# Negated scores, one joined map, and sliced head norms between attention rounds

## The reference, cut to what matters

```
logits = einsum('bqhmd,bkhmd->bhmqk', q_blk, k) + bias      # m = 0, 1: two maps a head
p = softmax(logits)
attn = p[:, :, 0] - lam * p[:, :, 1]
o = einsum('bhqk,bkhd->bqhd', attn, v)                      # 128 columns a head
o = o * rsqrt(mean(o * o, axis=-1) + 1e-5) * subln_g * (1 - lam_init)
```

```
score = where(admissible, einsum(w, relu(q_idx @ k_idx)), -inf);  sel = top_k(score, 128)
p = softmax(q . k[sel] / 8);           y_a = p @ v[sel]
qb, kb = rms_norm(qb, qn_b), rms_norm(kb, kn_b)            # per head of 64 columns
p = softmax(qb . kb / 8 + bias);       y_b = p @ vb
```

## Time and profile before

| | us |
|---|---|
| median of three runs | 4347.05 |
| span of the profiled execution | 4333.6 |
| PE busy in it | 3912.4 (90%) |
| DVE busy | 1669.4 (39%) |
| ACT busy | 1415.7 (33%) |
| POOL busy | 1391.7 (32%) |

### The profile page before, as it was taken

One profiled execution on the slowest core, in us unless ns is written; L12 is line 12 of the kernel. 1 busy time (PEld: TensorE's weight loads), 2 busy tenths in 40 slices (PEclk: granted clock), 3 DMA queues, 4 the chain that ended last, 5 costly groups with the idle time before them and its releaser, 6 DMA issues.

```text
span 4333.6 us, 66123 instructions
## 1 busy us (share of the span) xinstructions
PE 3912.4 (90%) x28400; PEld 3137.0 (72%) x28400; DVE 1669.4 (39%) x2914; ACT 1415.7 (33%) x2424; POOL 1391.7 (32%) x583
## 2 busy tenths in 40 slices
PE   7898789989989897989999979889899898898999
PEld 5687568878766786668777867668688676676887
DVE  4443340367133443241465147633211357322112
ACT  3344152222223343252222223442322224533222
POOL 4000324434333001314444434214344344033443
PEclk9899799999999998999999989989999999899999
DMA  3000212247321001212265222012222221121222
GB/s 131 2 3 5 80 43 99 96 166 255 110 78 39 3 3 41 76 49 97 78 244 197 93 78 78 30 49 98 92 91 85 97 78 39 40 92 67 95 97 97
DMA packets 37147, 356.59 MB, mean 82 GB/s; under 512 B 4224, under 2 KB 4352, under 8 KB 17920
## 3 DMA queue, kind: packets, MB, share of 16 engines
q1 hardware_dynamic: 19584, 278.93, 17.3%
q10 hardware_dynamic: 17280, 73.48, 4.8%
HBM read 350.29 MB, written 2.10 MB: 81 GB/s over the span
## 4 chain that ended last, share of the span: by engine, by line
PE 80%; DVE 11%; ACT 4%; issue 2%; POOL 1%; DMA 1%; POOLq 0%; DVEq 0%; PEldq 0%; ACTq 0%; SPq 0%; PEld 0%
PE bank L683 21%; PE bank L684 21%; PE bank L685 21%; PE bank L1013 12%; PE bank L1989 3%; ACT arena L2139 2%; ACT arena L1343 1%; DVE arena L1788 1%; DVE arena L1691 1%; DVE arena L2454 1%; DVE arena L2453 1%; DVE x L1851 1%; DMA ring<-stream 1%; POOL small L2299 1%; ACT hi_ring L762 1%
## 5 line engine op out<-in xcount | busy, mean ns | idle before, releaser
L771 POOL TENSOR_TENSOR ring_r<-ring,hi_ring 128x1024 fp32r<-128x1024 f32 (+1 forms) x522 | 1278.1, 2453 | 2556.1 <-ACT hi_ring L762 2556.1
L683 PE MATMUL bank<-xT_r,ring_r 128*128 128x512 f32 x2288 | 924.1, 404 | 24.0 <-DVE x_lo_r L2525 17.7
L684 PE MATMUL bank<-x_lo_r,hi_ring 128*128 128x512 f32 x2288 | 911.2, 398 | 0.0
L685 PE MATMUL bank<-xT_r,hi_ring 128*128 128x512 f32 x2288 | 906.7, 396 | 0.0
L762 ACT ACTIVATE hi_ring<-ring 128x1024 fp32r<-128x1024 f32 (+1 forms) x522 | 543.8, 1046 | 797.1 <-PE bank L685 356.1
L683 PEld LDWEIGHTS bank<-xT_r,ring_r 128*128 128x128 f32 x2288 | 440.0, 192 | 132.7 <-issue 31.3
L685 PEld LDWEIGHTS bank<-xT_r,hi_ring 128*128 128x128 f32 x2288 | 437.2, 191 | 102.7
L684 PEld LDWEIGHTS bank<-x_lo_r,hi_ring 128*128 128x128 f32 x2288 | 439.4, 192 | 95.5 <-issue 1.8
L1013 PE MATMUL bank<-arena 64*64 64x64 f32 (+4 forms) x7456 | 397.2, 250 | 77.6 <-DVE arena L1691 29.6
L1343 ACT ACTIVATE arena<-bank 128x512 f32<-128x512 f32 (+1 forms) x422 | 230.6, 548 | 568.7 <-PE bank L685 360.8
L1013 PEld LDWEIGHTS bank<-arena 64*64 64x64 f32 (+2 forms) x7456 | 307.4, 140 | 134.4 <-issue 91.6
(11 more groups left out here) (250 smaller groups left out, 5038.5 us busy)
## 6 DMA issues: line engine op xcount, KB each, us to landing
ring<-stream SPq DMA_DIRECT2D x132, 2048.0 KB, 7.8
arena<-ada ACTq DMA_DIRECT2D x96, 512.0 KB, 4.4
arena<-ln_rows ACTq DMA_DIRECT2D x5, 1024.0 KB, 7.6
arena<-edge ACTq DMA_DIRECT2D x4, 1024.0 KB, 5.0
arena<-edge ACTq DMA_DIRECT2D x2, 1792.0 KB, 7.6
arena<-pack ACTq DMA_DIRECT2D x2, 1485.0 KB, 6.1
arena<-pack ACTq DMA_DIRECT2D x2, 1200.5 KB, 12.6
x<-x_in SPq DMA_DIRECT2D x4, 512.0 KB, 7.4
```

Of the source, the lines that this page charges most:

```text
L683: first = nc.tensor.matmul(out_, left[1], right[0], start=start, stop=False)
L684: low = nc.tensor.matmul(out_, left[0], right[1], start=False, stop=False)
L685: return first, low, nc.tensor.matmul(out_, left[0], right[0], start=False, stop=stop)
L771: nc.gpsimd.tensor_tensor(feed.raw(n, ring_r), feed.raw(n), feed.hi(n).bitcast(F32), ALU.subtract).then_inc(split_lo, 1)
```

## The change

In block 1 and block 2, DVE's reduction now writes the negated sum of score and bias and keeps its minimum, which is the negated maximum; the separate negation goes, and ACT's exponential takes a scale of -1 and waits for the bank to be drained. In block 1 map 0 is no longer scaled: map 1 is scaled by -lambda times the ratio of the two row sums and added, and the missing factor is applied when ACT copies the output out of PSUM. ACT's Square of each output with its row sum goes; in its place `att_norm` begins with one Square of all 2048 columns on ACT and one reduction on DVE. In block 2 only 4 of the 18 steps of the last search stand ahead of the attentions, and the others follow one a round in rounds 0 to 13. The head norm of qb goes into rounds 0 to 10; kb's squares are in rounds 5 to 8 (before 1, 3, 5, 7), its eps in 9 (before 8), its multiplications in 12 to 15 (before 10 to 13), and it has cells of its own for the sums.

```diff
...
@@ -73,6 +73,7 @@
 FT2 = 22
 TOPK = 128
 TOP_STEPS = TOPK // 8 + 2
+TOP_EARLY = 4
 HQ = 8
 NEG = -1.0e30
 TAKEN = -3.0e38
@@ -445,10 +446,6 @@
             add("rows_T", name, c, banks=(banks[c % len(banks)],))
     rest = [(name, i, tt) for name in ("qb", "kb", "vb") for i in range(4) for tt in range(TT)]
 
-    def head_late(what, proj, n):
-        for tt in range(n):
-            add("head_" + what, proj, tt)
-
     def more(n):
 
         for name, i, tt in rest[:n]:
@@ -483,29 +480,27 @@
             add("idx", qt, h, banks=(h % 2,))
             if h in (3, 5):
                 more(1)
-        for i in range(TOP_STEPS if qt < TT - 1 else TOP_STEPS // 2):
+        for i in range(TOP_STEPS if qt < TT - 1 else TOP_EARLY):
             add("top", qt, i)
         more((10, 18, len(rest))[qt - 1])
-    head_late("sq", "qb", TT)
-    add("head_eps", "qb", banks=("power",))
-    head_late("mul", "qb", TT)
 
     def attend(a):
         for n in range(2):
             add("s_qk", a, n, banks=(2 + n,))
-        top, part = TOP_STEPS // 2, 16 * a
+        top, part = TOP_EARLY, 16 * a
         for n in range(TT * HQ + 3):
             if n < TT * HQ:
                 add("s_soft", a, n)
-            while a == 0 and top < min(TOP_STEPS, TOP_STEPS // 2 + TOP_STEPS * (n + 1) // 28):
+            while a == 0 and top < min(TOP_STEPS, TOP_EARLY + n + 1):
                 add("top", TT - 1, top)
                 top += 1
-            if a == 0 and n in (1, 3, 5, 7):
-                add("head_sq", "kb", n // 2)
-            if a == 0 and n == 8:
-                add("head_eps", "kb", banks=("power",))
-            if a == 0 and n in (10, 11, 12, 13):
-                add("head_mul", "kb", n - 10)
+            for proj, at_ in (("qb", 0), ("kb", 5)) if a == 0 else ():
+                if at_ <= n < at_ + TT:
+                    add("head_sq", proj, n - at_)
+                if n == at_ + TT:
+                    add("head_eps", proj, banks=("power",))
+                if at_ + 7 <= n < at_ + 7 + TT:
+                    add("head_mul", proj, n - at_ - 7)
             if 2 <= n < TT * HQ + 2:
                 add("s_tr", a, n - 2, banks=((4, 0)[n % 2],))
             if part < (16, 24)[a]:
@@ -938,6 +933,7 @@
     o_tok = region(20388, TT)
     prob = [region(a_, 2) for a_ in (22436, 23460, 8548, 9572)]
     probT = region(24484, 2)
+    o_squares = region(24484, TT)
     pool_tmp = region(25508, 2, S + 2 * PAD)
     merged = region(10664, DT)
     gates = region(14760, DT)
@@ -961,7 +957,8 @@
     subln_s = tiny(1)
     neg_lam = tiny(4)
     row_sum = tiny(2 * 16)
-    row_max = tiny(2 * 16)
+    minus_max = tiny(2 * 16)
+    power_kb = tiny(32)
     row_w = tiny(2 * 16)
     sq_sum = tiny(32)
     power = tiny(32)
...
@@ -1459,10 +1456,10 @@
                 f(v[:, i, :], bank[b][:, :], ACT.Copy).then_inc(bank_free[b], 1)
             elif name == "att_soft":
                 i = args[0]
-                act.wait_ge(scores_ready, i + 1)
                 for m in range(2):
                     k = 2 * i + m
-                    ins = f(prob[i % 4][:, m, :], prob[i % 4][:, m, :], ACT.Exp, bias=row_max[:, k:k + 1],
+                    drained(act, uses, "att_qk", i, only=m)
+                    ins = f(prob[i % 4][:, m, :], prob[i % 4][:, m, :], ACT.Exp, bias=minus_max[:, k:k + 1], scale=-1.0,
                             accum_out=row_sum[:, k:k + 1])
                 ins.then_inc(exp_done, 1)
             elif name == "att_tr":
@@ -1473,8 +1470,11 @@
                 i = args[0]
                 h, qt = i // TT, i % TT
                 filled(b, n)
-                f(pool_tmp[:, i % 2, 0:P], bank[b][:, 0:P], ACT.Square, accum_out=sq_sum[:, i:i + 1])
-                f(o_tok[:, qt, h * P:(h + 1) * P], bank[b][:, 0:P], ACT.Copy).then_inc(bank_free[b], 1)
+                f(o_tok[:, qt, h * P:(h + 1) * P], bank[b][:, 0:P], ACT.Copy, scale=row_w[:, 2 * i:2 * i + 1]).then_inc(bank_free[b], 1)
+            elif name == "att_norm":
+                for i in (DH * TT - 2, DH * TT - 1):
+                    drained(act, uses, "att_pv", i)
+                f(o_squares.rearrange("p t c -> p (t c)"), o_tok.rearrange("p t c -> p (t c)"), ACT.Square).then_inc(o_squared, 1)
             elif name == "att_out":
                 h = args[0]
                 filled(b, n)
@@ -1786,28 +1786,26 @@
                     filled(banks[m], use[m])
                     at_ = (TT - 1 - qt) * P
                     V.tensor_tensor_reduce(out=prob[i % 4][:, m, :], in0=bank[banks[m]][:, :], in1=rel[:, h, at_:at_ + S],
-                                           scale=1.0, scalar=-3.0e38, op0=ALU.add, op1=ALU.max,
-                                           accum_out=row_max[:, k:k + 1]).then_inc(bank_free[banks[m]], 1)
-                again(banks[1], use[1])
-                V.tensor_scalar(row_max[:, 2 * i:2 * i + 2], row_max[:, 2 * i:2 * i + 2], -1.0, None, ALU.mult)\
-                    .then_inc(scores_ready, 1)
+                                           scale=-1.0, scalar=3.0e38, op0=ALU.add, op1=ALU.min,
+                                           accum_out=minus_max[:, k:k + 1]).then_inc(bank_free[banks[m]], 1)
             elif name == "att_tr":
                 i = args[0]
                 dve.wait_ge(exp_done, i + 1)
                 w = row_w[:, 2 * i:2 * i + 2]
                 link(V.reciprocal(w, row_sum[:, 2 * i:2 * i + 2]))
-                link(V.tensor_tensor(w[:, 1:2], w[:, 1:2], neg_lam[:, 0:1], ALU.mult))
+                link(V.scalar_tensor_tensor(out=w[:, 1:2], in0=w[:, 1:2], scalar=neg_lam[:, 0:1], in1=row_sum[:, 2 * i:2 * i + 1],
+                                            op0=ALU.mult, op1=ALU.mult))
                 p0, p1 = prob[i % 4][:, 0, :], prob[i % 4][:, 1, :]
-                link(V.tensor_scalar(p0, p0, w[:, 0:1], None, ALU.mult))
                 V.scalar_tensor_tensor(out=p0, in0=p1, scalar=w[:, 1:2], in1=p0, op0=ALU.mult, op1=ALU.add)\
                     .then_inc(prob_ready, 1)
             elif name == "att_norm":
-                for i in (DH * TT - 2, DH * TT - 1):
-                    drained(dve, uses, "att_pv", i)
-                V.tensor_scalar(power[:, 0:16], sq_sum[:, 0:16], 1.0 / P, 1e-5, ALU.mult, ALU.add).then_inc(stats_ready, 1)
+                dve.wait_ge(o_squared, 1)
+                link(V.tensor_reduce(power[:, 0:16].rearrange("p (t h) -> p t h", t=TT),
+                                     o_squares.rearrange("p t (h c) -> p t h c", h=DH), AX.X, ALU.add))
+                V.tensor_scalar(power[:, 0:16], power[:, 0:16], 1.0 / P, 1e-5, ALU.mult, ALU.add).then_inc(stats_ready, 1)
                 dve.wait_ge(power_ready, n + 1)
                 V.tensor_tensor(o_tok.rearrange("p t (h c) -> p t h c", h=DH), o_tok.rearrange("p t (h c) -> p t h c", h=DH),
-                                power[:, 0:16].rearrange("p (h t) -> p t h", h=DH).unsqueeze(3).to_broadcast([P, TT, DH, P]),
+                                power[:, 0:16].rearrange("p (t h) -> p t h", t=TT).unsqueeze(3).to_broadcast([P, TT, DH, P]),
                                 ALU.mult).then_inc(o_scaled, 1)
             elif name == "branch":
                 k, dt = args
...
@@ -2226,8 +2223,8 @@
                 a, i = args
                 qt, h = i // HQ, i % HQ
                 w = (qt + 1) * P
-                act.wait_ge(score2_ready, a * TT * HQ + i + 1)
-                f(prob2[a][:, i % 4, 0:w], prob2[a][:, i % 4, 0:w], ACT.Exp, bias=row_max[:, i:i + 1],
+                drained(act, uses, "s_qk", a, i)
+                f(prob2[a][:, i % 4, 0:w], prob2[a][:, i % 4, 0:w], ACT.Exp, bias=minus_max[:, i:i + 1], scale=-1.0,
                   accum_out=sum2[:, i:i + 1]).then_inc(exp2_done, 1)
             elif name == "s_tr":
                 a, i = args
@@ -2294,7 +2291,7 @@
             if "power" not in banks:
                 return
             n = use[banks.index("power")]
-            cell = power[:, args[1]:args[1] + 1] if name == "rms" else power[:, 0:width[args[0]]]
+            cell = power[:, args[1]:args[1] + 1] if name == "rms" else (power_kb if args[0] == "kb" else power)[:, 0:width[args[0]]]
             pool.wait_ge(stats_ready, n + 1)
             nc.gpsimd.tensor_tensor(cell, cell, half_minus.to_broadcast([P, cell.shape[1]]), ALU.pow).then_inc(power_ready, 1)
         return step
...
@@ -2382,16 +2383,17 @@
             elif name == "head_sq":
                 proj, tt = args
                 dve.wait_ge(sums_sq, 2 + TT * HEADS_LATE.index(proj) + tt)
-                link(V.tensor_reduce(power[:, tt * HQ:(tt + 1) * HQ], stage_sq[proj][:, tt, :].rearrange("p (h c) -> p h c", h=HQ),
+                link(V.tensor_reduce(power_of(proj)[:, tt * HQ:(tt + 1) * HQ], stage_sq[proj][:, tt, :].rearrange("p (h c) -> p h c", h=HQ),
                                      AX.X, ALU.add))
             elif name == "head_eps":
-                V.tensor_scalar(power, power, 1.0 / CH, EPS2, ALU.mult, ALU.add).then_inc(stats_ready, 1)
```

(21 more changed lines are left out.)

## The result

The changed kernel takes 4299.07 us (median of 4 executions, 4292.79 to 4306.14), the one before 4346.57 (median of 4): a ratio of 0.9894 (95% interval 0.988 to 0.9908), 47.5 us faster. A second comparison gave 4299.89 against 4343.51, 43.6 faster. The two intervals put the gain between 39 and 52 us. Forecast was 4313, 34.2 us faster, with a range down to 4302: the direction and most terms were right, the gain was larger than the range allowed.

A forecast was written before the change was run, and what follows sets the result against it. Mostly PE matmuls bound the kernel, with DVE pacing block 1's rounds; only stretches where PE waits change. Block 2's -30.0 and block 1's -4.2 make -34.2 us: 4313, with 4302 to 4331 holding about 8 in 10.

The forecast's parts named there:

- Block 2's start: Block 2's first reduction, freed of five search steps and qb's norm, starts at 2720.2 instead of 2736.61: -16.4 us.
- The first 14 rounds: Block 2's first 14 rounds take on moved search and norm work: 39.0 us, against 34.9 today.
- Block 1's rounds: Block 1's attention: the period falls from 2.99 us to PE's 2.60, bounds 2.30 and 2.75.
- Block 1's norm: Behind block 1's rounds, ACT's Square and DVE's reduction now stand bare ahead of the power: +4.1 us per layer.
- Block 1 in all: Block 1's rounds and norm together: -2.1 us per layer, -4.2 for both, bounds +3 and -13.
- A: Block 2, round 10: kb's power holds qb's multiplication 3.4 us, twice; 4320 us, chance 0.12.
- B: Block 2's first 14 rounds: DVE idles 6.3 us again; 4322, or 4325 with the negation's gain halved; chance 0.14.
- C: Block 1's rounds: scores pack tighter, period falls to DVE's 2.3; 4301 us with no idle in block 2; chance 0.10.
- D: Block 2's first 14 rounds: the loop goes in series with the moved work; slower, 4360 us, chance 0.05.
- Block 2, the later rounds: Block 2's chain from 2772 to 2896 loses the negation 15 times at 0.18: 2.7 us per layer, bounds 0 and 3.5.
- My +4.1: Growth forecast for block 2's first 14 rounds, from 34.9 us today to 39.0.
- the closing step: End of block 2's search, counted as DVE work in the first 14 rounds: 2.7 us, 2.22 and a short one.

The follow-up runs named there:

- its experiment: Block 1's part of the change alone, block 2 as before, against the kernel before: 4339.46 us, ratio 0.9992 (0.9983 to 1.0002).
- the spread search: Changed kernel with five search steps ahead of block 2's first scores, the other thirteen at three for five rounds: 4294.6 us, ratio 0.9892.

## Why the prediction missed

**Right in place and size.** *Block 2's start*: -16.4 forecast. The first reduction comes 22.1 us earlier than before, of which 5.7 were there already (the first search's first `MAX8` starts at 2644.39 instead of 2650.05), so -16.4. *The first 14 rounds*: 39.0 forecast, 38.03 measured; DVE's work 37.0 forecast, 36.71 measured. PE's busy time in them didn't shrink as the forecast said: the clock rose from 0.83 to 0.96, but 166 matmul records fall into the stretch instead of 145, and 32.35 became 34.04. *Block 1's rounds*: 2.60 forecast, 2.63 measured, set by PE as said, though PE's wait for the joining instruction isn't gone but stands in every other round. *Block 1's norm*: +4.1 forecast; PE's wait grew from 6.30 to 10.38, by 4.1. Block 1 in all -2.1 per layer forecast; from the first reduction to the output transposes it is 56.96 before and 54.86 after, -2.1, and -4.05 for both layers by its experiment's medians. Two outer bounds of the working are added up wrong (2 × 8.0 is 16, not 18, for block 2; 2 × 6.0 is 12, not 13, for block 1); neither entered the range.

**Rivals.** A, B, C and D fell. *A*: kb's power and qb's fourth multiplication did meet, in both layers, and the power held nothing:

```profile
2741.16 5.42 POOL L2296 TENSOR_TENSOR small<-small 128x32 f32<-128x32 f32 x1 [0.78 <-DVE small L2390]
...
2742.84 0.69 DVE L2396 TENSOR_TENSOR arena<-arena,small 128x512 f32<-128x512 f32 x1
```

*B*: DVE idles 1.3 of 38.0, not 6.3. *C*: the steady rounds of block 1 take 2.65, not 2.3. *D*: no loop in series; a pair of those rounds takes 5.4 us (38.03 / 7), where it took 5.0.

**The step that failed** is "Block 2, the later rounds": "The chain from 2772 to 2896 passes through it 15 times: 15 × 0.18 = 2.7 per layer (bounds 0 and 3.5; the other rounds are PE's)". The term was too small, so was its upper bound, and PE's clock in these rounds had no term at all. In the profiled executions the rounds behind the 15th reduction are 7.0 and 10.4 us shorter. Over all executions profiled, the last 32 rounds take 67.4 on the mean of ten stretches with the negation (62.7 to 70.6), and 62.8 on the mean of sixteen without (59.1 to 67.3): -4.6 per layer. Nine of the 15 passes lie in these rounds, -1.6. Over two layers 5.9 us are missing here.

A second, smaller part is in the first 32 rounds as a whole: 80.84 before, 81.46 after, so +0.6. My +4.1 less the other six passes (1.1) gives +3.0: 2.4 per layer, 4.8 in all. Per layer 1.0 of that is the first 14 rounds (39.0 for 38.03: 1.3 of waits where I allowed 2.0), and 1.4 lies in rounds 15 to 32 (45.96 to 43.43, 2.5 where 1.1 was counted). The negation by itself is worth 1.2 there (45.96 to 44.80 with it alone removed), as counted, so the rest of the 2.5 came with the moves, which also shift PE's products across the cut at the 15th reduction. With 5.9 this makes 10.7, and the medians moved 9.4 to 13.3 more than the 34.2 forecast.

What the runs put in the place of 15 × 0.18: the negation's full price in block 2 is 13.3 us without the moves (it alone removed) and 18.2 with them (put back). The forecast had 2 × 2.7 for it, and had left 14 more per layer, 2 × 2.5, out of its count of DVE's work in the first 14 rounds. Of the 18.2, 5.9 lie in the first 14 rounds of the two layers (40.87 and 41.12 with it, 38.03 without) and 3.5 in rounds 15 to 32 (45.95 and 44.40 against 43.43 and 43.46), which leaves some 9 for the last 32.

Two things make up the 4.6 per layer in the last 32 rounds. The loop is shorter: 2.1 us at like clock by the line through all stretches (0.5 to 3.4 by single pairs), not far from the 1.6 of the nine passes. The rest goes with the granted clock, which was 0.88 on the mean without the negation against 0.82 with it. That the clock rises when the negation goes is borne out by whole launches (0.9497 on nine executions with it alone removed, 0.9472 on nineteen before), though not by every stretch: the ranges overlap (0.77 to 0.97 and 0.76 to 0.92), and with the negation only in the second attention it stood at 0.92 and 0.90. By which step a shorter loop raises the clock no run shows. What is shown is that this one stretch varies by 8 us at the same code, and that its length goes with its clock.

**What is no cause.** The 13.4 us between span and median were let stand, so the forecast is a difference, 34.2, and the result is 40.9 between the profiled spans and 43.6 and 47.5 between medians. In every execution that lists both, the time is 1.8 to 1.9 us above the span; so some 11.6 of the 13.4 say that the profiled execution of before was a quick one, as the changed kernel's was by 4.6 (4294.47 against 4299.07). The forecast's range ended 45 us under the median of before. How much of the 3 us beyond it is the luck of four executions (they spread by 13 us) can't be told; the 9 to 13 us between forecast and result are more than that luck.

## What to carry to other kernels

A chain of waits counts the passes of one execution. Removing an instruction from a loop between engines can also pay in passes that the chain didn't choose, so the upper bound at a fixed clock is all its passes, not the fifteen seen (argued here, not tested by itself); and it can change the clock of the engine that the loop feeds, which in the last 32 rounds here went with about half of the gain. Where a stretch runs below full clock, compare it at like clock over several executions before an edit is priced by it. And when a stretch stands bare behind a stage, look first for independent work that may go ahead of it: moving the output transposes of four heads behind three gates brought 21 us, shortening what they waited for 8.

## What the hardware showed

An elementwise pass of GpSimd and a power of GpSimd act differently on DVE. Beside the pass that starts at 2731.69, a multiplication of 0.69 took 1.83, and ended 0.55 behind it:

```profile
2731.69 2.38 POOL L766 TENSOR_TENSOR ring_r<-ring,hi_ring 128x1024 fp32r<-128x1024 f32 x1
...
2732.08 0.68 DVE L2456 MATCH_REPLACE8 arena<-arena 128x512 f32<-128x512 f32 x1
...
2732.79 1.83 DVE L2396 TENSOR_TENSOR arena<-arena,small 128x512 f32<-128x512 f32 x1
```

Beside the power of 5.42 it kept its 0.69 (above). The Trainium skill, page "SBUF — State Buffer", section "SBUF: two separate sides", says that a GpSimd instruction that reads SBUF and a DVE instruction with two SBUF inputs exclude each other for the whole of the one that starts first. The trace agrees for the pass (2.38) and not for the power, which reads SBUF too; there the measurement decides.

An instruction with one SBUF input can be held as well. The search's closing step took 2.27 beside a pass of the changed kernel:

```profile
2748.71 2.44 POOL L766 TENSOR_TENSOR ring_r<-ring,hi_ring 128x1024 fp32r<-128x1024 f32 x1 [2.13 <-ACT hi_ring L757]
...
2749.16 2.27 DVE L2458 TENSOR_SCALAR arena<-arena 128x512 f32<-128x512 f32 x1
```

With the spread search it falls where GpSimd is idle, and takes 0.42:

```profile
2767.32 0.42 DVE L2458 TENSOR_SCALAR arena<-arena 128x512 f32<-128x512 f32 x1
```

In the kernel before it took the forecast's 2.22 at 2766.86, beside a pass of 2.36 that starts at 2766.43. So 1.8 of the 2.2 us that the forecast counted as the closing step's work was a wait. Not every one-input instruction is held: the MATCH_REPLACE8 of the same width at 2732.08, inside the pass of 2731.69, took 0.68, as it does elsewhere.
